# Convolution's input chunks: 512 moving columns, and an adder on GpSimd

## The reference, cut to what matters

```
ple_gate = sigmoid(rms_norm(h, ple_norm) @ w_ple_gate)
h = h + ple_gate * (p @ w_ple_proj)                      # end of the first block

def short_conv_mixer(h, w_in, conv_w, w_out):            # start of the second block
    b_gate, c_gate, u = jnp.split(h @ w_in, 3, axis=-1)  # h is normed; w_in is 1024 x 3072
    v = c_gate * u
    vp = jnp.pad(v, ((0, 0), (CONV_WIDTH - 1, 0), (0, 0)))
    conv = sum(conv_w[k] * vp[:, k:k + S] for k in range(CONV_WIDTH))   # 3 taps
    return (b_gate * conv) @ w_out
```

## Time and profile before

| | us |
|---|---|
| three executions | 1198.78, 1199.07, 1199.53 |
| the profiled execution, its own time | 1203.85 |
| its span (first to last instruction) | 1202.0 |
| PE busy | 1191.4 (99%) |
| DVE busy | 867.7 (72%) |
| ACT busy | 646.0 (54%) |
| POOL busy | 220.7 (18%) |
| mean granted TensorE clock | 0.997 |

### The profile page before, as it was taken

One profiled execution on the slowest core, in us unless ns is written; L12 is line 12 of the kernel. 1 busy time (PEld: TensorE's weight loads), 2 busy tenths in 40 slices (PEclk: granted clock), 3 DMA queues, 4 the chain that ended last, 5 costly groups with the idle time before them and its releaser, 6 DMA issues.

```text
span 1202.0 us, 19528 instructions
## 1 busy us (share of the span) xinstructions
PE 1191.4 (99%) x7801; PEld 1063.2 (88%) x7802; DVE 867.7 (72%) x1199; ACT 646.0 (54%) x868; POOL 220.7 (18%) x110
## 2 busy tenths in 40 slices
PE   9999999999999999999999999999999999999997
PEld 6888888988899888888999988888899878888886
DVE  6877667788868877766788786655688777766553
ACT  6655444475655755545643555543446784655441
POOL 1443301000000334310000025510000240454000
PEclk9999999999999999999999999999999999999999
DMA  8555555962345555555545555555576305655540
GB/s 317 210 176 189 196 176 176 280 210 107 105 150 176 177 206 178 194 191 186 180 160 179 194 198 199 180 205 180 197 255 245 106 2 175 210 179 200 182 175 36
DMA packets 31569, 217.53 MB, mean 181 GB/s; under 512 B 3584, under 2 KB 3856, under 8 KB 6272
## 3 DMA queue, kind: packets, MB, share of 16 engines
q1 hardware_dynamic: 30000, 210.33, 50.3%
q0 software_dynamic: 1344, 5.53, 1.6%
q10 hardware_dynamic: 144, 0.52, 0.1%
HBM read 215.30 MB, written 4.22 MB: 183 GB/s over the span
## 4 chain that ended last, share of the span: by engine, by line
PE 93%; DVE 4%; ACT 1%; DMA 1%; issue 1%; POOL 0%; DVEq 0%; SPq 0%; ACTq 0%; POOLq 0%
PE bank L1561 42%; PE bank L1562 21%; PE bank L1554 7%; PE bank L1555 7%; PE bank L1556 7%; DVE w_hl L814 1%; DMA raw<-weights 1%; PE bank L1962 1%; ACT w_hl L417 1%; PE bank L1734 1%; PE bank L1856 0%; PE bank L1670 0%; PE bank L1839 0%; PE bank L2009 0%; PE bank L1875 0%
## 5 line engine op out<-in xcount | busy, mean ns | idle before, releaser
L814 DVE TENSOR_TENSOR w_hl<-raw,w_hl 128x2048 fp32r<-128x2048 f32 x194 | 444.1, 2289 | 117.8 <-ACT w_hl L417 116.8
L417 ACT ACTIVATE w_hl<-raw 128x2048 fp32r<-128x2048 f32 x195 | 370.5, 1902 | 115.0 <-PE bank L1562 66.4
L1561 PE MATMUL bank<-x_hl,w_hl 128*128 128x512 f32 x908 | 318.2, 396 | 0.1
L1561 PE MATMUL bank<-hidden,w_hl 128*128 128x512 f32 x832 | 289.8, 395 | 0.0
L368 POOL TENSOR_TENSOR hidden<-hid_f,hidden 128x256 fp32r<-128x256 f32 (+1 forms) x76 | 189.6, 2494 | 521.0 <-ACT hidden L500 306.9
L1562 PE MATMUL bank<-x_hl,w_hl 128*128 128x256 f32 x908 | 253.0, 279 | 0.0
L1562 PE MATMUL bank<-hidden,w_hl 128*128 128x256 f32 x832 | 231.1, 278 | 0.0
L1561 PEld LDWEIGHTS bank<-x_hl,w_hl 128*128 128x128 f32 x908 | 170.4, 188 | 40.9 <-issue 0.6
L1561 PEld LDWEIGHTS bank<-hidden,w_hl 128*128 128x128 f32 x832 | 156.1, 188 | 36.8
L1562 PEld LDWEIGHTS bank<-x_hl,w_hl 128*128 128x128 f32 x908 | 170.9, 188 | 0.1
L478 ACT ACTIVATE second<-bank 128x512 f32<-128x512 f32 (+1 forms) x107 | 57.1, 534 | 202.4 <-PE bank L1562 202.3
(11 more groups left out here) (385 smaller groups left out, 1537.4 us busy)
## 6 DMA issues: line engine op xcount, KB each, us to landing
raw<-weights SPq DMA_DIRECT2D x197, 1024.0 KB, 4.9
bias_skew<-bias_rows POOLq DMA_DIRECT2D x1, 3072.0 KB, 27.4
gate_or_bias<-bias_skew POOLq DMA_DIRECT2D x1, 2048.0 KB, 10.0
h<-x_t SPq DMA_DIRECT2D x2, 512.0 KB, 5.7
out_t<-out_g SPq DMA_DIRECT2D x4, 256.0 KB, 2.5
con<-consts SPq DMA_DIRECT2D x1, 769.5 KB, 12.4
raw<-weights ACTq DMA_DIRECT2D x1, 512.0 KB, 5.5
raw<-weights SPq DMA_DIRECT2D x1, 512.0 KB, 7.0
```

The source lines that it names most:

```text
L417: nc.scalar.activation(dst, src, ACT.Copy).then_inc(hi_split, 1)
L814: V.tensor_tensor(w_lo[:, s, :], raw[:, s, :], w_hi[:, s, :].bitcast(F32), ALU.subtract).then_inc(lo_split, 1)
L1561: mm(out_, w_hi[:, s, c:c + m], x, start=start, stop=False, **kw)
```

## The change

The convolution's chunks are now written with `wide` to two banks each: (0, 1), (2, 3) and (4, 5). ScalarE copies both banks of a chunk (1024 columns) to SBUF, to one of three places conv_x (the two halves of sq and the tile second), GpSimd adds the second half of each bank to the first in place (512 columns), and VectorE reads the sums from SBUF. Two semaphores are new: conv_out_of (ScalarE to GpSimd and TensorE) and conv_sum (GpSimd to VectorE). A chunk's banks are free after the copy; a place conv_x is free after VectorE has read it (drained). In the PLE stage the gate chunks now go to banks 0, 2, 4, 6 and the projection to banks 1, 3, 5, 7 (before 0 to 3 and 4 to 7), and the sum of squares to bank 6 (before 3).

```diff
@@ -91,6 +91,7 @@
 ACC, TURN, SUMS = 0, 4, 7
 OUT_BANKS = ((0, 1), (2, 1), (6, 1), (0, 0))
+CONV_BANKS = ((0, 1), (2, 1), (4, 1))
 NSA_OUT_BANKS = ((3, 1), (6, 1), (0, 1), (2, 0))
 HID = {"ffn1": 0, "ffn2": FF, "mlp0": 2 * FF, "mlp1": 2 * FF + MF}
 UPS = {"ffn1": FF, "ffn2": FF, "mlp0": MF, "mlp1": MF}
@@ -220,6 +221,7 @@
             sem("s_z"), sem("s_abs"), sem("s_min"), sem("s_ln"), sem("s_l"), sem("s_e"), sem("s_x"), sem("s_a"),
             sem("s_pv"))
         merged_done = sem("merged_done")
+        conv_out_of, conv_sum = sem("conv_out_of"), sem("conv_sum")
         masks = sem("masks")
         ple_sig = sem("ple_sig")
         bias_ready, bias_out, bias_in = sem("bias_ready"), sem("bias_out"), sem("bias_in")
@@ -297,6 +299,9 @@
         f_ms, f_r0, f_t, f_r = (stat[:, 2 * i:2 * i + 2] for i in range(4))
         f_all = bank[:, SUMS, S:2 * S]
+        conv_x = [sq_flat[:, 0:1024], sq_flat[:, 1024:2048], second_flat]
+        conv_x = [two(t) for t in conv_x]
+
         def gate_parts(s):
             both = w_hi[:, s, 0:KT * P].rearrange("p (k b n) -> p k b n", k=KT, b=2)
@@ -384,6 +389,10 @@
             pool.dma_start(heads[:, 0:2, :], p_t).then_inc(p_in, 16)
             pool.wait_ge(p_in, 16)
             low("ffn2")
+            for n in range(12):
+                x = conv_x[n % 3]
+                pool.wait_ge(conv_out_of, n + 1)
+                nc.gpsimd.tensor_tensor(x[:, :, 0:S], x[:, :, 0:S], x[:, :, S:2 * S], ALU.add).then_inc(conv_sum, 1)
             low("mlp0")
             pool.wait_ge(chunk_used, C["mlp0"] + 2 * MF)
@@ -680,13 +689,23 @@
             nxt(c0)
             rsqrt("mix0", load=False)
+            def conv_copy(j, i):
+
+                act.wait_ge(chunk_used, i * 3 + (c0 + j + 1))
+                if not isinstance(i, int):
+                    act.wait_ge(drained, i * 3 + (DRAIN["conv"] + j - 2))
+                b = CONV_BANKS[j][0]
+                nc.scalar.activation(conv_x[j], bank[:, b:b + 2, :], ACT.Copy).then_inc(conv_out_of, 1)
+
             def conv_turn(i):
-                if not isinstance(i, int):
-                    nxt_in(c0, 0, i, 3)
-                nxt_in(c0, 1, i, 3)
-                act.wait_ge(conv_full, i + 1)
-                nc.scalar.activation(y_h[:, bass.ds(i * 2, 2), :], y_f[:, bass.ds(i * 2, 2), :], ACT.Copy).then_inc(op_hi, 1)
-                nxt_in(c0, 2, i, 3)
+                for j in range(3):
+                    conv_copy(j, i)
+                    if j == 2:
+                        act.wait_ge(conv_full, i + 1)
+                        nc.scalar.activation(y_h[:, bass.ds(i * 2, 2), :], y_f[:, bass.ds(i * 2, 2), :],
+                                             ACT.Copy).then_inc(op_hi, 1)
+                    if j > 0 or not isinstance(i, int):
+                        nxt_in(c0, j, i, 3)
             conv_turn(0)
             with act.Fori(1, 4) as i:
@@ -1251,18 +1270,18 @@
             downs("ffn2", 0.5, "ple", y_h, y_l)
-            factor("ple", 3)
+            factor("ple", 6)
             for j in range(4):
                 y, hj = y_f[:, 2 * j:2 * j + 2, :], h[:, 2 * j:2 * j + 2, :]
                 dve.wait_ge(chunk_used, PLE_GATE[j] + 1)
-                V.tensor_tensor(y, two(bank[:, ACC + j, :]), r_two, ALU.mult).then_inc(ple_raw, 1)
+                V.tensor_tensor(y, two(bank[:, 2 * j, :]), r_two, ALU.mult).then_inc(ple_raw, 1)
                 if j >= 1:
                     operand_piece("mix0", x_h, x_l, j - 1)
                 else:
                     nxt(PLE_GATE[0])
                     dve.wait_ge(chunk_used, C["ple_proj"] + 1)
                 dve.wait_ge(ple_sig, j + 1)
-                st.done(V.tensor_tensor(y, two(bank[:, 4 + j, :]), y, ALU.mult))
+                st.done(V.tensor_tensor(y, two(bank[:, 2 * j + 1, :]), y, ALU.mult))
                 V.tensor_tensor(hj, hj, y, ALU.add).then_inc(h_upd, 1)
                 if j == 0:
                     nxt(C["ple_proj"])
@@ -1284,9 +1303,9 @@
                 st.n = i * 8 + n
                 for j in range(2):
-                    dve.wait_ge(chunk_used, i * 3 + (c0 + j + 1))
-                    st.done(V.tensor_tensor(t_ab[:, j, :], bank[:, TURN + j, 0:S], t_m[:, :], ALU.mult))
-                    V.tensor_tensor(v_pad[:, j, 2:S + 2], t_ab[:, j, :], bank[:, TURN + j, S:2 * S],
+                    dve.wait_ge(conv_sum, i * 3 + (j + 1))
+                    st.done(V.tensor_tensor(t_ab[:, j, :], conv_x[j][:, 0, 0:S], t_m[:, :], ALU.mult))
+                    V.tensor_tensor(v_pad[:, j, 2:S + 2], t_ab[:, j, :], conv_x[j][:, 1, 0:S],
                                     ALU.mult).then_inc(drained, 1)
                     dve.wait_ge(drained, i * 3 + (DRAIN["conv"] + j + 1))
                     for k in range(3):
@@ -1300,8 +1319,8 @@
                                                            in1=hid_f[:, j, :], op0=ALU.mult, op1=ALU.add))
                     if j == 1 or not isinstance(i, int):
                         nxt_in(c0, j, i, 3)
-                dve.wait_ge(chunk_used, i * 3 + (c0 + 3))
-                V.tensor_tensor(t_ab[:, :, :], two(bank[:, TURN + 2, :]), r_two, ALU.mult).then_inc(drained, 1)
+                dve.wait_ge(conv_sum, i * 3 + 3)
+                V.tensor_tensor(t_ab[:, :, :], conv_x[2][:, :, 0:S], r_two, ALU.mult).then_inc(drained, 1)
                 dve.wait_ge(drained, i * 3 + (DRAIN["conv"] + 3))
                 V.tensor_tensor(y_f[:, bass.ds(i * 2, 2), :], t_ab[:, :, :], hid_f[:, :, :],
                                 ALU.mult).then_inc(conv_full, 1)
@@ -1903,30 +1922,31 @@
             pe.wait_ge(h_upd, UPD["ple"] - KT + 6)
             project("ple_gate0", [0], y_hl, "ple")
-            sum_squares(6, 3)
+            sum_squares(6, 6)
             arrived(C["ple_proj"] + 1)
             for o in range(KT):
                 for k in range(2):
-                    last = product(bank[:, 4 + o // 2, (o % 2) * S:(o % 2) * S + S], C["ple_proj"] % RING,
+                    last = product(bank[:, 1 + o // 2 * 2, (o % 2) * S:(o % 2) * S + S], C["ple_proj"] % RING,
                                    k * D + o * P, P, x_hl[:, k, :, :], k == 0, k == 1)
             last.then_inc(chunk_used, 1)
             for j in range(1, 4):
                 arrived(PLE_GATE[j] + 1)
                 if j == 3:
                     pe.wait_ge(ms_ready, NO["ple"] + 1)
-                pair(PLE_GATE[j] % RING, j, y_hl).then_inc(chunk_used, 1)
+                pair(PLE_GATE[j] % RING, 2 * j, y_hl).then_inc(chunk_used, 1)
             c = C["conv_in"]
-            two_pairs(c, ((TURN, 0), (TURN + 1, 0)), x_hl, "mix0", 3, between=lambda: sum_squares(7))
+            two_pairs(c, CONV_BANKS, x_hl, "mix0", 3, between=lambda: sum_squares(7))
             arrived(c + 3)
-            pair((c + 2) % RING, TURN + 2, x_hl).then_inc(chunk_used, 1)
+            out_chunk(CONV_BANKS[2], (c + 2) % RING, x_hl)
             with pe.Fori(1, 4) as i:
                 for j in range(3):
                     arrived(i * 3 + (c + j + 1))
-                    pe.wait_ge(drained, i * 3 + (DRAIN["conv"] + j - 2))
-                    pair((c + j) % RING, TURN + j, x_hl).then_inc(chunk_used, 1)
+                    pe.wait_ge(conv_out_of, i * 3 + (j - 2))
+                    out_chunk(CONV_BANKS[j], (c + j) % RING, x_hl)
             c = C["conv_out"]
+            pe.wait_ge(conv_out_of, 11)
             two_pairs(c, OUT_BANKS, y_hl, "conv", 3)
             for j in range(2, 4):
                 arrived(c + j + 1)
```

## The result

The changed kernel takes 1211.37 us (median of four executions, 1210.58 to 1212.68); before it is 1199.08 (1198.78 to 1199.53). The ratio is 1.0088, 95% interval [1.0068, 1.0108]: it is slower, by 12.3 us between the medians. The prediction was 1210.9, range 1202.0 to 1214.5.

A forecast was written before the change was run, and what follows sets the result against it. TensorE was taken to bind the kernel. VectorE would be later by 3.3 + 3 x 3.5 = 13.8 us, less 2.0 spare: 11.8 us on the median 1199.07 gives 1210.9 us, range 1202.0 to 1214.5.

The forecast's parts named there:

- held both ways: Convolution: GpSimd's additions and VectorE's instructions with two SBUF inputs hold each other; 11.8 us slower, 1210.9, chance 0.67.
- no holding: Rival: additions run beside VectorE in 1.04 to 1.3 us without holding; 0.9 to 2.4 us faster, chance 0.08.
- Half held: Rival: GpSimd waits for VectorE but not the reverse, only chunk 0's addition serial; 1.9 us slower, 1201.0, chance 0.11.
- In the gaps: Rival: most additions run while VectorE waits for ScalarE; 3 to 6 us slower, 1202 to 1205, chance 0.14.
- TensorE's step: Convolution's 192 steps, each 0.007 to 0.014 us cheaper: 1.3 to 2.7 us less, not subtracted in the sum.
- ScalarE's copies: Twelve copies of 1024 columns, 1.0 us each, fitting into ScalarE's waits: counted at nothing.
- The tail after VectorE's low part: Chunk 0's addition ends 1.16 us after VectorE's low part, VectorE goes on 0.10 later: 1.3 us a turn.
- A held instruction: Additions for chunks 1 and 2 each hold a VectorE instruction with SBUF inputs for 1.1 us.
- The turn: One turn of VectorE's convolution loop: the three additions cost 3.5 us together, against 0.9 us spare.
- Turn 0: First turn: two additions fall into the Newton step, the third into tile 0; 3 x 1.1 = 3.3 us.
- the spare time: VectorE's lead over TensorE's need at the convolution's end, 2.0 us, taken off VectorE's delay.
- The signs: What would show it, including TensorE's low-part waits of 3 to 4 us first, then near 3 a turn.

The follow-up runs named there:

- e1: Changed kernel with GpSimd adding only one column of each tile, copies and hand-overs kept: 1200.99 us, 1.0002 of the kernel before.
- e3: Changed kernel with a GpSimd memset of the 1024 columns of each copy in place of the addition: 1199.08 us, 0.9989 of the kernel before.
- e5: Changed kernel with VectorE reading first halves from PSUM, copies and whole additions running beside with VectorE waiting for no sum: 1208.22 us, 1.0067 of before.
- e4: Changed kernel without copies and additions, VectorE reading the first halves of the banks from PSUM: 1200.07 us, 1.0004 of the kernel before.
- e10: Changed kernel with each GpSimd addition of 512 columns cut into two of 256: 1211.19 us, 1.0085 of the kernel before.

## Why the prediction was right, by its steps

**The mechanism** was that of the forecast: held both ways. Rival "no holding" is what e1 and e3 run into once the reading is gone. "Half held" (1.9 slower) falls with e5, where VectorE waits for nothing of GpSimd's and is late all the same. "In the gaps" (3 to 6 slower) falls with the rows of the changed kernel: in each of turns 1 to 3 VectorE waits 1.18 for the first addition and is held 0.90 to 1.09 by each of the other two.

**TensorE's step.** 0.353, the slower of the two paces given; its gain is in no sum, rightly (e4).

**ScalarE's copies.** 1.01 us each against 1.0, at nothing: shown by e1. TensorE waits for the low part, not for a copy, also before conv_out, where the profile names the copy.

**The tail after VectorE's low part.** 1.16 against 1.16. L1307 waits 1.18, just under the 1.2 to 1.4 asked for; from the start of the low part to the start of L1307 it is 654.27 - 650.80 = 3.47 where it was 2.21, so the turn loses 1.26 by it, against the sum's 1.3.

**A held instruction.** 0.90 and 1.08 in the turn shown, 0.90 to 1.11 in all nine, against 1.1, which was scaled from one row of 0.54. That was the step with the thinnest support. That it came near is in part luck.

**The turn.** 19.74 - 16.39 = 3.35 against 3.5. Turn 0: held 1.11, 0.98 and 1.09, together 3.2 against 3.3. VectorE's low part of conv_out's second chunk comes 683.75 - 601.06 = 82.69 us after the convolution's start, before 69.88: 12.8 later against 13.8. TensorE goes on with that chunk at 686.10, 85.04 after the start, before at 677.60, 74.15 after it: 10.9 later against 11.8. The difference of the two is 1.9, so the spare time was about 2.0, as read. The term that came out too big is the holding: nine held instructions make 9.2 us and not 9.9.

**From the stretch to the time.** 11.8 was forecast and 12.3 measured between medians, with 10.84 in the stretch; the interval of the ratio (8.2 to 13.0) holds both. The medians of all experiments but e3 lie above their stretches, too, by up to 2.7 us (e10: 11.3 and 8.60), and what makes that up was not found. The forecast for the profiled execution, 1215.7, missed: its own time is 1210.58. The profile of before held 4 us that aren't the change's doing: `wide` at 0.353 a step in ffn1, where the changed kernel's profile has 0.347 (2.4 us), and a fall of the clock in the attention (about 1.6 us). Setting the sum against the median, as the prediction did for its number, took care of that.

**The signs.** TensorE's first wait is 3.40 (3 to 4 asked for). From 660.49 to 680.20, three chunks, it takes 19.71 us where 48 steps of 0.353 make 16.94, so it waits 2.8 a turn (near 3 asked for).

**Where it was wrong.** It wanted the granted clock unchanged. During TensorE's first wait, of 3.40 us, the clock fell to half (stretch: us, PE busy, PEld, DVE, ACT, POOL, PEclk, DMA share, GB/s):

```profile
620.00:628.00 8.00, 4.59 (x25) 3.77 (x24) 7.65 (x12) 0.00 (x0) 0.92 (x1) 0.88 0.00 0
628.00:631.00 3.00, 3.00 (x11) 2.59 (x10) 1.33 (x2) 2.33 (x2) 0.00 (x0) 0.50 0.82 273
631.00:634.00 3.00, 3.00 (x14) 2.57 (x13) 2.29 (x1) 2.81 (x3) 1.91 (x1) 0.68 0.18 76
634.00:637.00 3.00, 3.00 (x19) 2.58 (x18) 1.86 (x5) 1.08 (x2) 0.57 (x1) 1.00 0.77 257
```

0.50 is 1.2 GHz of 2.4. Steps took 0.64 from 627.44 on, about eight of them, 2.4 us lost. At 653.15 TensorE waits for a low part again (0.39), and so it would have come no further by then at the full clock: the end hardly feels the fall. This is worked out from the rows and not tried.

## What to carry to other kernels

An addition on GpSimd with operands in SBUF isn't beside VectorE's work but in it: count most of its length (here 0.9 to 1.3 us of VectorE's time for 512 columns, 0.69 on VectorE itself) against VectorE's spare time, also where nobody waits for its result. What matters is where both engines read: instructions of VectorE that read one operand from PSUM passed (e5), and moving its inputs from PSUM to SBUF took that away. Leaving them in PSUM isn't enough, since the next instructions of a tile read SBUF: e5's stretch is still 6.44 longer. And a cheaper step on the bounding engine is worth nothing if the next engine has 0.9 us a turn to spare and is given 3.35 more.

At the pace of 0.353 no version with two banks wins much here: with the adding left out altogether (e4) the stretch is 0.93 us shorter.

## What was not expected of the hardware

- A GpSimd memset of 1024 columns (0.96 us) ran beside a VectorE instruction with two SBUF inputs without either being longer (e3), while an addition of two columns stood 1.3 us (e1).
- VectorE's TENSOR_SCALAR with its one tensor in SBUF is held as well: 0.58 instead of 0.35 in e10. The same section of the Trainium skill names tensor_scalar among the operations that can take the shared ports; this row agrees.
- The clock's fall to half in TensorE's wait of 3.40 us. In the experiments TensorE's waits in the stretch were 2.8 us or shorter, and the granted clock was 1.00 from 600 to 700 us in all ten. One profile shows this fall; that the length of the wait alone decides was not tried.
- The same `wide` code runs at 0.347 or at 0.353 a step, steady within a stage and different between stages and executions. What picks the pace stays open.
